# Indexer scores of the sample group: own keys only, in column groups

## What is computed

```python
s = jnp.einsum('bqhd,bsd->bqhs', qi_blk, ki_all).astype(jnp.float32)   # 8 heads of 64
score = jnp.einsum('bqhs,bqh->bqs', jax.nn.relu(s), w_blk.astype(jnp.float32))
score = jnp.where(key_pos[None, None, :] <= p_blk[None, :, None], score, -jnp.inf)
_, idx = lax.top_k(score, ksel)
```

## Time and profile before

| | us |
|---|---|
| median of 3 runs | 3032.91 |
| lowest, highest | 3031.16, 3038.57 |
| the profiled execution | 3032.8 |
| its span | 3031.0 |
| PE, VectorE, ScalarE busy | 2847.6, 1713.7, 975.2 |

### The profile page before, as it was taken

One profiled execution on the slowest core, in us unless ns is written; L12 is line 12 of the kernel. 1 busy time (PEld: TensorE's weight loads), 2 busy tenths in 40 slices (PEclk: granted clock), 3 DMA queues, 4 the chain that ended last, 5 costly groups with the idle time before them and its releaser, 6 DMA issues. The chain is left out here.

```text
span 3031.0 us, 49959 instructions
## 1 busy us (share of the span) xinstructions
PE 2847.6 (94%) x21584; PEld 2696.5 (89%) x21584; DVE 1713.7 (57%) x2587; ACT 975.2 (32%) x1303; POOL 185.6 (6%) x209
## 2 busy tenths in 40 slices
PE   8999989989999999999999899899899999999997
PEld 7988888988889898899999888899798999989996
DVE  1464387667666747445434545765777657564444
ACT  1433242223343332233224233322333423322332
POOL 0000000000100003100000100000000000040000
PEclk9999999999999999999999899999999999999999
DMA  6765453464756557665556744443756565576652
GB/s 200 199 186 167 125 139 105 119 167 132 205 143 181 141 165 208 190 179 169 152 157 197 209 139 124 119 122 105 184 150 187 158 172 140 157 234 174 173 157 81
DMA packets 831148, 485.76 MB, mean 160 GB/s; under 512 B 26132, under 2 KB 812820, under 8 KB 829938
## 3 DMA queue, kind: packets, MB, share of 16 engines
q1 hardware_dynamic: 808880, 407.71, 49.0%
q0 software_dynamic: 20448, 68.92, 7.2%
q10 hardware_dynamic: 1600, 5.93, 0.6%
HBM read 466.28 MB, written 16.47 MB: 159 GB/s over the span
## 5 line engine op out<-in xcount | busy, mean ns | idle before, releaser
L627 PE MATMUL mb<-xsplit,wsplit 128*128 128x264 f32 (+1 forms) x5312 | 1579.3, 297 | 34.7 <-DVE wsplit L1486 27.5
L628 PE MATMUL mb<-xsplit,wsplit 128*128 128x264 f32 (+1 forms) x5312 | 1524.0, 287 | 0.0
L629 PE MATMUL mb<-xsplit,wsplit 128*128 128x264 f32 (+1 forms) x5312 | 1522.0, 287 | 0.0
L627 PEld LDWEIGHTS mb<-xsplit,wsplit 128*128 128x128 f32 (+1 forms) x5312 | 1015.9, 191 | 66.8 <-issue 45.6
L628 PEld LDWEIGHTS mb<-xsplit,wsplit 128*128 128x128 f32 (+1 forms) x5312 | 1015.9, 191 | 8.7 <-issue 3.8
L629 PEld LDWEIGHTS mb<-xsplit,wsplit 128*128 128x128 f32 (+1 forms) x5312 | 1010.5, 190 | 1.1
L1486 DVE TENSOR_TENSOR wsplit<-ring,wsplit 128x1024 fp32r<-128x1024 f32 (+2 forms) x664 | 777.0, 1210 | 206.0 <-ACT wsplit L1215 193.5
L1215 ACT ACTIVATE wsplit<-ring 128x1024 fp32r<-128x1024 f32 (+2 forms) x664 | 662.7, 1043 | 135.9 <-PE mb L629 111.0
L1242 ACT ACTIVATE gbuf<-mb 128x264 f32<-128x264 f32 x160 | 62.6, 391 | 847.3 <-PE mb L629 822.2
L643 PE MATMUL mb<-work,bring 128*128 128x264 f32 x1280 | 310.6, 385 | 0.0
L1516 DVE TENSOR_TENSOR gbuf<-gbuf,mb 128x264 f32<-128x264 f32 x128 | 54.9, 429 | 401.9 <-PE mb L643 399.9
(11 more groups left out here) (455 smaller groups left out, 2165.4 us busy)
## 6 DMA issues: line engine op xcount, KB each, us to landing
ring<-in_w_in_dram SPq DMA_DIRECT2D x592, 512.0 KB, 4.7
bring<-in_w_branch_dram SPq DMA_DIRECT2D x160, 256.0 KB, 3.5
ring<-in_w_out_dram SPq DMA_DIRECT2D x64, 512.0 KB, 4.6
ring<-in_w_mem_kv_dram SPq DMA_DIRECT2D x32, 512.0 KB, 3.5
work<-in_cache_mem_k_dram POOLq DMA_DIRECT2D x16, 512.0 KB, 5.4
work<-in_cache_mem_v_dram POOLq DMA_DIRECT2D x16, 512.0 KB, 4.5
work<-in_state_gdn_dram POOLq DMA_DIRECT2D x8, 512.0 KB, 5.1
out_s_gdn_dram<-work POOLq DMA_DIRECT2D x8, 512.0 KB, 4.4
```

Of the source, the lines that this page charges most:

```text
L627: pe.matmul(bank[0:n, 0:T], wh, ah, start=first, stop=False)
L628: pe.matmul(bank[0:n, 0:T], wh, al, start=False, stop=False)
L629: mm = pe.matmul(bank[0:n, 0:T], wl, ah, start=False, stop=last)
```

## The change

A round now takes two pages of each sample instead of an eighth of all pages. Partition p stands for sample p // 16, the first or second of the two pages, and a piece of 16 tokens of it. The page numbers for the gathers are worked out at the layer's start for that (the small page-number column ptf is gone, with its transfer). Queries are laid out as 16 columns a sample, and each sample's queries meet its own 128 columns of keys only: eight matmuls with 32 columns of weights (its own 16 and the next 16) in four column groups, two samples in each. VectorE clamps and weighs two blocks of 128 columns with one weight a partition (wcol), written so that the pieces lie together. Two matmuls of eight columns give the scores of the round in bank 3, where those of all rounds collect. After the loop VectorE puts them in order, PE transposes them once, and VectorE copies them to scs; four k-steps stand ahead of each of PE's two waits for that. VectorE no longer copies scores in a round.

In this layout a partition of scs holds every second token of two neighbouring pages. So the numbering of equal keys needs counts over pairs of partitions (the tables pairs_of and earlier2, one more matmul of 129 columns, three more operations on VectorE), and the row numbers of the keys are worked out for it. The mask "earlier" moves from step 13 to step 1. New small tables stand in the constants; the table of semaphore counts is changed to fit and not shown.

```diff
@@ -262,7 +262,14 @@
-add("last_page", np.stack([i % NPG == NPG - 1, np.where(i % NPG == NPG - 1, 0.0, LOWEST), i], 1))
+add("last_page", np.stack([i % NPG == NPG - 1, np.where(i % NPG == NPG - 1, 0.0, LOWEST)], 1))
+add("token", (2 * (i % 64))[:, None])
+add("second", (i % NPG // 8)[:, None])
+add("piece", (i % 8)[:, None])
+add("first_of_two", -(i % 2 == 0)[:, None].astype(np.float32))
+add("per_key", (i[:, None] // 32 == np.arange(8)[None] // 2) & (i[:, None] % 32 // 8 == np.arange(8)[None] % 2))
+add("quarter", np.tile(np.eye(4), (2, 1)))
+add("half", np.repeat(np.eye(2), 4, 0))
...
@@ -342,7 +349,7 @@
-pti = merged[:, 0, 0:1 + NB * NPG].bitcast(I32)
+pti = merged[:, 0, 0:NB * NPG].bitcast(I32)
...
@@ -416,6 +422,7 @@
+x1 = zarea(3072 + 512, P)
...
@@ -500,9 +507,13 @@
-Qblk = sb("Qblk", [P, P])
+Qblk = sb("Qblk", [P, P + 16])
 ptB = sb("ptB", [P, NB * NPG])
-mws = sb("mws", [P, P])[:, :]
+wcol = sb("wcol", [P, 2])[:, :]
+pairs_of = memkv[:, 9 * WIDE + 3 * P:9 * WIDE + 4 * P]
+earlier2 = memkv[:, 9 * WIDE + 4 * P:9 * WIDE + 5 * P]
+halved = memkv[:, 9 * WIDE + 5 * P:9 * WIDE + 5 * P + 64]
+pairs = memkv[:, 6 * WIDE:7 * WIDE]
...
@@ -706,7 +717,8 @@
-pe.matmul(bb[:, 1, 481:482], earlier, cnt[:, 1:2], start=True, stop=True).then_inc(sem.tk_mm, 1)
+pe.matmul(bb[:, 1, 481:482], earlier2, cnt[:, 1:2], start=True, stop=True)
+pe.matmul(bb[:, 1, P:P + WIDE], pairs_of, equal, start=True, stop=True).then_inc(sem.tk_mm, 1)
...
@@ -861,7 +873,7 @@
-mm = pe.matmul(bb[:, 0, 0:P], lw, tb("blk_pages")[0:NB, :], start=True, stop=True)
+mm = pe.matmul(bb[:, 0, 0:2], lw, tb("half")[0:NB, :], start=True, stop=True)
...
@@ -878,15 +890,22 @@
-    for u in range(2):
-        mm = pe.matmul(bb[:, 2 + u, :], Qblk[:, :], ikT[:, u * 512:(u + 1) * 512], start=True, stop=True)
+    for b in range(NB):
+        p0, c0 = 32 * (b % 4), P * (b // 4)
+        mm = pe.matmul(bb[p0:p0 + 32, 2, c0:c0 + P], Qblk[:, 16 * b:16 * b + 32],
+                       ikT.rearrange("p (u x) -> p u x", x=P)[:, :, 16 * b:16 * b + 16], start=True, stop=True)
     mm.then_inc(sem.ik_mm, 1)
     fill(6)
     pe.wait_ge(sem.ik_rel, base.ik_rel + j + 1)
-    for u in range(8):
-        mm = pe.matmul(bb[:, 0, 2 * u:2 * u + 2], ikr[:, u * P:(u + 1) * P], tb("parity"), start=True, stop=True)
+    for h in range(2):
+        c0 = 16 * j + 8 * h
+        mm = pe.matmul(bb[:, 3, c0:c0 + 8], ikr[:, h * P:(h + 1) * P], tb("per_key"), start=True, stop=True)
     mm.then_inc(sem.ik_sc, 1)
-    pe.wait_ge(sem.sc_ok, base.sc_ok + j + 1)
+fill(4)
+pe.wait_ge(sem.sc_ok, base.sc_ok + 1)
+pe.transpose(bb[:, 3, P:2 * P], x1, ident).then_inc(sem.ik_sc, 1)
+fill(4)
+pe.wait_ge(sem.sc_ok, base.sc_ok + 2)
...
@@ -1279,8 +1298,7 @@
-act.dma_start(pti[:, 0:1], pt.rearrange("(p o) -> p o", o=1)).then_inc(sem.pages_in, 16)
-act.dma_start(pti[:, 1:], pt.partition_broadcast(P)).then_inc(sem.pages_in, 16)
+act.dma_start(pti, pt.partition_broadcast(P)).then_inc(sem.pages_in, 16)
...
@@ -1539,9 +1557,8 @@
-dve.wait_ge(sem.pages_in, 32)
-dve.tensor_copy(ptf, pti[:, 0:1])
-v(dve.tensor_copy(ptB[:, :], pti[:, 1:]))
+dve.wait_ge(sem.pages_in, 16)
+v(dve.tensor_copy(ptB[:, :], pti))
...
@@ -1554,6 +1571,12 @@
+v(dve.tensor_tensor(earlier.rearrange("p (b g) -> p b g", b=NB), tb("strict_t").rearrange("p (b g) -> p b g", b=NB),
+                    bc(tb("page_of"), NPG), ALU.mult))
+v(dve.tensor_reduce(halved, ident.rearrange("p (q k) -> p q k", k=2), AX.X, ALU.add))
+v(dve.tensor_copy(pairs_of.rearrange("p (q k) -> p q k", k=2), bc(halved, 2)))
+v(dve.tensor_tensor(earlier2, earlier, pairs_of, ALU.mult))
+v(dve.tensor_tensor(earlier2, earlier, earlier2, ALU.subtract))
...
@@ -1581,15 +1604,16 @@
-v(dve.tensor_tensor(earlier.rearrange("p (b g) -> p b g", b=NB), tb("strict_t").rearrange("p (b g) -> p b g", b=NB),
-                    bc(tb("page_of"), NPG), ALU.mult))
 dve.tensor_reduce(cnt[:, 0:2], memkv[:, 2 * WIDE:4 * WIDE].rearrange("p (n x) -> p n x", n=2), AX.X, ALU.add)\
     .then_inc(sem.tk_ok, 1)
 yield
 dve.wait_ge(sem.tk_mm, base.tk_mm + n + 3)
 v(dve.tensor_scalar(need, bb[:, 1, 480:481], -1.0, float(KS), ALU.mult, ALU.add))
 v(dve.tensor_copy(eoff, bb[:, 1, 481:482]))
-v(dve.tensor_tensor_scan(order, ones[:, 0:1].to_broadcast([P, WIDE]), equal, eoff, ALU.mult, ALU.add))
+v(dve.tensor_copy(pairs, bb[:, 1, P:P + WIDE]))
+v(dve.tensor_tensor_scan(order, ones[:, 0:1].to_broadcast([P, WIDE]), pairs, eoff, ALU.mult, ALU.add))
+v(dve.tensor_tensor(pairs, pairs, equal, ALU.subtract))
+v(dve.scalar_tensor_tensor(order, pairs, tb("first_of_two"), order, ALU.mult, ALU.add))
...
@@ -1628,8 +1652,15 @@
-v(dve.tensor_scalar(goff[:, 8:9], ptf, 8.0, float(l * n_pool * 8), ALU.mult, ALU.add))
-v(dve.tensor_scalar(goff[:, 0:8], tb("iota")[:, 0:8], goff[:, 8:9], None, ALU.add))
+of_all = work[:, 0:P].rearrange("p (b g) -> p b g", b=NB)
+mine = work[:, P:P + NPG]
+v(dve.tensor_tensor(of_all, ptB[:, :].rearrange("p (b g) -> p b g", b=NB), bc(tb("page_of"), NPG), ALU.mult))
+v(dve.tensor_reduce(mine, of_all.rearrange("p b g -> p g b"), AX.X, ALU.add))
+two_pages = mine.rearrange("p (j t) -> p j t", t=2)
+v(dve.tensor_tensor(goff[:, 0:8], two_pages[:, :, 1], two_pages[:, :, 0], ALU.subtract))
+v(dve.scalar_tensor_tensor(goff[:, 0:8], goff[:, 0:8], tb("second"), two_pages[:, :, 0], ALU.mult, ALU.add))
+v(dve.tensor_scalar(goff[:, 8:9], tb("piece"), float(l * n_pool * 8), None, ALU.add))
+v(dve.tensor_scalar(goff[:, 0:8], goff[:, 0:8], 8.0, goff[:, 8:9], ALU.mult, ALU.add))
...
@@ -1766,9 +1797,10 @@
+v(dve.memset(lw, 0.0))
 for k in range(2):
-    mm = dve.tensor_tensor(lw[:, 64 * k:64 * k + 64].rearrange("p (b h) -> p b h", b=NB), bh(wts, NB),
-                           tb("blk_heads")[0:NB, :].rearrange("p (b h) -> p b h", b=NB), ALU.mult)
+    mm = dve.tensor_tensor(lw.rearrange("p (c s h) -> p c s h", c=4, s=4)[:, :, k, :], bh(wts, 4),
+                           bc(tb("quarter")[0:NB, :], IH), ALU.mult)
...
@@ -1777,9 +1809,9 @@
-    v(dve.tensor_copy(Qblk[half, 64 * k:64 * k + 64].rearrange("p (b h) -> p h b", b=NB),
+    v(dve.tensor_copy(Qblk[half, 0:P].rearrange("p (b k h) -> p k h b", b=NB, k=2)[:, k],
                       bb[half, 3, 0:64].rearrange("p (h b) -> p h b", h=IH)))
-dve.tensor_copy(mws, bb[:, 0, 0:P]).then_inc(sem.qd_ok, 1)
+dve.tensor_copy(wcol, bb[:, 0, 0:2]).then_inc(sem.qd_ok, 1)
...
@@ -1792,11 +1824,20 @@
-    dve.scalar_tensor_tensor(ikr.rearrange("p (u x) -> p u x", u=8), bb[:, 2:4, :].rearrange("p s (u x) -> p (s u) x", x=P),
-                             0.0, bh(mws, 8), ALU.max, ALU.mult).then_inc(sem.ik_rel, 1)
-    dve.wait_ge(sem.ik_sc, base.ik_sc + j + 1)
-    dve.tensor_copy(scs[:, 16 * j:16 * j + 16], bb[:, 0, 0:16]).then_inc(sem.sc_ok, 1)
+    if j:
+        dve.wait_ge(sem.ik_sc, base.ik_sc + j)
+    for h in range(2):
+        c = slice(h * P, (h + 1) * P)
+        mm = dve.tensor_scalar(ikr[:, c].rearrange("p (g u) -> p u g", u=8), bb[:, 2, c].rearrange("p (u g) -> p u g", u=8),
+                               0.0, wcol[:, h:h + 1], ALU.max, ALU.mult)
+    mm.then_inc(sem.ik_rel, 1)
     stream(1)
+dve.wait_ge(sem.ik_sc, base.ik_sc + 8)
+dve.tensor_copy(x1.rearrange("p (b j k) -> p j b k", b=NB, j=8), bb[:, 3, 0:P].rearrange("p (j b k) -> p j b k", j=8, b=NB))\
+    .then_inc(sem.sc_ok, 1)
+dve.wait_ge(sem.ik_sc, base.ik_sc + 9)
+dve.tensor_copy(scs[:, 0:PAGE], bb[:, 3, P:2 * P]).then_inc(sem.sc_ok, 1)
+dve.wait_ge(sem.sc_ok, base.sc_ok + 2)
...
@@ -2090,8 +2131,15 @@
-v(dve.tensor_scalar(goff[:, 8:9], tb("last_page")[:, 2:3], float(l * n_pool * PAGE), None, ALU.add))
-v(dve.tensor_scalar(rowid, ptB[:, :], float(PAGE), goff[:, 8:9], ALU.mult, ALU.add))
+two_pages = ptB[:, :].rearrange("p (q t) -> p q t", t=2)
+page = own2[:, 0:64]
+v(dve.tensor_tensor(page, two_pages[:, :, 1], two_pages[:, :, 0], ALU.subtract))
+v(dve.scalar_tensor_tensor(page, page, tb("parity")[:, 1:2], two_pages[:, :, 0], ALU.mult, ALU.add))
+v(dve.tensor_scalar(goff[:, 8:9], tb("token"), float(l * n_pool * PAGE), None, ALU.add))
+for k in range(2):
+    if k:
+        v(dve.tensor_scalar(goff[:, 8:9], goff[:, 8:9], 1.0, None, ALU.add))
+    v(dve.tensor_scalar(rowid.rearrange("p (q k) -> p q k", k=2)[:, :, k], page, float(PAGE), goff[:, 8:9], ALU.mult, ALU.add))
...
```

More of the change, by code:

```diff
@@ L174, in last_stored @@
     return FREED[FIRST_RESULT[max(i for i in range(l * LEN, (l + 1) * LEN) if is_it(CHUNKS[i]))]][1]
-BEFORE = dict(x_in=32, pages_in=32, tables=16, x_T=KC, xh_ok=KC, x_ok=KC)
+BEFORE = dict(x_in=32, pages_in=16, tables=16, x_T=KC, xh_ok=KC, x_ok=KC)
 PER_LAYER = dict(
     param_T=1, mem_T=8, rows_mm=9, lg_mm=4, pT_mm=4, ov_mm=4, qr_mm=2, qb_mm=16, lt_mm=2, lpt_mm=2, sv_mm=18,
-    gt_mm=1, rot_mm=5, ki_mm=1, qd_mm=1, new_mm=1, ik_T=8, ik_mm=8, ik_sc=8, tk_mm=19, gc_mm=1, tails=4, ss=4,
+    gt_mm=1, rot_mm=5, ki_mm=1, qd_mm=1, new_mm=1, ik_T=8, ik_mm=8, ik_sc=9, tk_mm=19, gc_mm=1, tails=4, ss=4,
     tok_mm=2, kk_mm=1, inv_T=2, at_mm=2, y_mm=12, z_mm=12, u_mm=2, bt_mm=1, pt_mm=2, o_mm=2, qk_mm=2, sk_mm=16,
```

(3 more changed lines are left out.)

## The result

The changed kernel takes 3001.16 us (median of 4 runs, 3000.11 to 3004.33); the kernel before, on the same chip, 3032.03 us (4 runs, 3029.83 to 3038.57). The ratio is 0.9895, 95% interval 0.9884 to 0.9906: 1.05% faster. The forecast was 3000.2. The profiled execution has a span of 3000.2 us, 30.8 less than before.

What follows compares the result with a forecast made beforehand. PE's instruction stream bounds the kernel. Layer terms sum to -15.5 us, two layers -31.0; two clock dips gone (-3.1) and one new (+1.5) give -32.6 from 3032.8: 3000.2 us, range 2990 to 3012.

Steps and rivals of the forecast that it cites:

- The grouped products: In each round, eight 128-column products on four column groups take 0.77 us instead of L882's 1.72, saving 0.95 us.
- Rival (a): The grouped products do not overlap: 2.1 instead of 0.77 us a round, 21.6 us more, 3022; 4 in 100.
- Rival (b): Short runs or reloaded weights make grouped records twice the pitch or more: 3.3 us over forecast a round, 3052; 4 in 100.
- The sums: In each round, L887's 16 records become 4 at 0.46 us and the copy wait goes, saving 1.65 us.
- VectorE's passes: In each round, L1795's 1.23 us pass becomes two over 128 elements, at most 0.3 us each, hidden by six k-steps.
- (c): The shorter round uncovers ScalarE's copy, a gather or the splits, about 1 us a round: 3016; 7 in 100.
- (d): Weight supply sets the loop's time and the products go without effect: about 3031; 3 in 100.
- The new wait ahead of L931: Behind the loop, PE arrives early and waits 2.5 to 3 us for the decay chain, costing 2.9 us a layer.
- Step 1: Search step 1: five more VectorE operations, 1.6 us, make the splits 1.1 us later, costing PE 1.1 us a layer.
- The sign for the wait there: PE's wait for VectorE at the first convolution grows about 1.1 us, from 1.40 to 2.5 us.
- one new stretch in two layers: Behind the grown wait at the first convolution, one new clock dip in two layers, +1.5 us.
- Steps 13 and 14: Search: step 13 loses the mask product, 0.33 us less; step 14 gains pair-count work, 1.3 us more, a layer.

Runs made afterwards that it cites:

- e6: Changed kernel with two products of 512 columns over all queries in place of the eight grouped ones, most scores wrong; 3020.63 us, ratio 0.9954.
- e4: Changed kernel with all eight products of a round in the first column group, most scores wrong; 3023.62 us, ratio 0.9957.
- e5: Changed kernel with the eight products reading 128 neighbouring key columns instead of eight runs of 16, scores wrong; 2999.67 us, ratio 0.9874.
- e7: Changed kernel with each of the two sums over heads done four times, eight a round, same results; 3029.48 us, ratio 0.9979.
- e2: Changed kernel with the six operations building the search's tables moved from search step 1 into rounds 1 to 3 of the loop; 3004.45 us.
- e0: The changed kernel run once more without edits, as base for the runs beside it; 2999.63 us, ratio 0.9883.
- e1: Changed kernel without the two groups of four k-steps ahead of PE's waits for the scores at the loop's end; 3000.32 us, ratio 0.9892.

## Why the prediction was right

The grouped products were sized from L1035, the same form elsewhere in the kernel: 0.77 us forecast, 0.78 measured, and e6 confirms the difference to the whole products by itself. Rival (a), no overlap, is what e4 builds: its price of 1.35 us a round is 1.29. Rival (b) fell with e5: the runs cost nothing, as L1149 had said, and the 0.78 us leave no room for reloads of weights either. Against the column groups spoke the Trainium skill (TensorEngine Tiling (Array Packing), Tiling Modes: a change of mode drains TensorE). The row shows 0.22 us from the last k-step's record to L895, where e6's whole products start 0.12 us after theirs. So going over to the column groups costs about 0.1 us, inside the 0.78.

The sums are the one term of the round that was mis-sized: four records at 0.115 us each were 0.46, and they take 0.36 from start to start. The 0.115 was a time in flight over sixteen records, and not a distance between starts. 0.1 us in sixteen rounds is 1.6 us, most of what the loop gave beyond the forecast.

VectorE's passes were put at no more than 0.3 us each, by a pass of 0.29 us. They take 0.46 in the mean and 0.74 together. The forecast's row writes in order; these passes write with a stride of eight elements, and whether it is that or the kind of operation was not separated. Reading from bb is not it: the copy L1836 reads the same tile and writes runs of two elements in 0.29 us. It cost nothing, with 1.4 us of cover left. Rivals (c) and (d) are out by the same timeline: no wait in the round, and e7 shows that what is added to a round's products is added to the time. The price of (d) was wrong by the forecast's own terms: without the 41.6 us of the rounds its sum gives 3042 and not 3031, at the edge of slower.

The new wait ahead of L931 was forecast at 2.5 to 3 us and is 2.59. Step 1 was to cost 1.1 us and cost 1.00, and e2 takes exactly that back. The sign for the wait there was wrong in this profile: it was to grow from 1.40 to 2.5 us, and fell to 0.87. The step that failed is that PE would come to it at the same time as before; PE was slowed on the way by a stretch at 1.2 GHz behind the new wait of 2.59 us, inside a stretch that VectorE bounds. Where no such stretch came (e0 in layer 1, e1), the wait is 2.40 us. The forecast charged 1.5 us for one new stretch in two layers, behind the grown wait. In this profile none stands there, and those that came stand ahead of it; in e1 one does. None of them costs anything: the stretches take 20.47 and 15.14 us with and without. So that term was put in the wrong place and at the wrong price. Steps 13 and 14 are right to 0.1 us.

What was really missed is the clock. The forecast asked where waits grow and found the one at the first convolution. It did not ask this of the wait that it had itself put at 1.3 us in step 14, and this one brought 1.5 us a layer right behind the next wait, and more further on. Net, the clock took some 6 us outside the counted places where 1.5 were forecast; an earlier start gave 1.0, and the rounds and their surroundings gave 1.8 more than forecast. The errors partly cancel: the profiled execution lies 1.8 us above the forecast. The median of the kernel before came out 0.9 us lower with one more run than in the forecast, so that the 1 us between 3000.2 and 3001.16 is partly luck. The range, 2990 to 3012, had its upper part for added dips and holds all medians of the unchanged form (3001.16, 2999.63, 3000.56).

## What to carry to other kernels

Size a new form of product by the same form elsewhere in the trace, from the start before it to the second start behind it, so that switches and restarts are inside the figure; that gave 0.77 for 0.78 us. Take each wait that an edit adds, however short, to the place where PE stands next at a long wait, and look there for room for the clock to fall: a microsecond of work ahead of PE cost six here. And judge edits of a few microseconds by the windows of their own stretch; the median of a whole execution moved by 5 to 13 us with where the clock fell.

## What the runs showed of the hardware

- The same 1.0 us of VectorE's work in each layer, added or taken away, moved the median by 10.7 (with a product of 0.33 us on PE besides) and 13.4 us, as PE's clock fell in other places, most of them far behind the edit. Over the whole execution 0.976 against 0.970 of full clock is all that the cores' view shows of it.
- A stretch at 1.2 GHz cost nothing where VectorE decides, as long as PE had a wait left to give: e0's two windows behind the loop take 20.47 us each, at a clock of 0.92 with a wait of 0.86 us and at 1.00 with one of 2.40. In layer 1 of e2 PE had none left, and it cost 0.1 us.
- Taking eight k-steps away ahead of two short waits brought a stretch at 1.2 GHz that took back 1.7 of the 2 us.
- Of 32 VectorE passes over 128 elements with strided writes the mean is 0.46 us, against 0.29 for one in order:

```profile
L1831 DVE TENSOR_SCALAR work<-bb,wcol 128x128 f32<-128x128 f32 x32 | 11.9, 462 | 73.4 <-PE bb L895 73.4
```

- Why e7's runs lie 8 us above what its rounds add over e5, whose span its profile exceeds by just that, stays open; so does which of the waits set the places of the other stretches at 1.2 GHz. A version with k-steps ahead of the right two waits was not tried.
